# Loads and stores one a slot, four units split twice, weight sums on VectorE instead of GpSimd

## What is computed

```python
mod = silu(c) @ w_ada + b_ada; shift, scale, gate = split(mod, 3)
h = rmsnorm(x, g_pre) * (1 + scale) + shift
p = h @ w_in                                  # 1024 x 8704, the bulk of the work
y_pool = pool_mixer(a_in) * silu(a_g)
y_hgrn = hgrn2_mixer(b_q, b_f, b_i) * silu(b_g)
y_conv = short_conv_mixer(c_x, c_b, c_c) * silu(c_g)
y_diff = diff_attention(d_q, d_k, d_v) * silu(d_g)
merged = sum(sigmoid(m_g[i]) * (y_i @ w_merge_i))
x = x + gate * rmsnorm(merged @ w_out, g_post)
```

## Time and profile before

| what | value |
|---|---|
| median of 3 runs | 2409.23 us (2408.41 to 2409.46) |
| time of the profiled execution | 2409.45 us |
| its span, first to last instruction | 2407.7 us |
| PE, PEld busy | 2245.6 us (93%), 1857.7 us (77%) |
| DVE, ACT, POOL busy | 1474.8, 1122.4, 847.1 us |
| DMA | 569.99 MB, mean 237 GB/s |

### The profile page before, as it was taken

One profiled execution on the slowest core, in us unless ns is written; L12 is line 12 of the kernel. 1 busy time (PEld: TensorE's weight loads), 2 busy tenths in 40 slices (PEclk: granted clock), 3 DMA queues, 4 the chain that ended last, 5 costly groups with the idle time before them and its releaser, 6 DMA issues. The chain is left out here.

```text
span 2407.7 us, 35100 instructions
## 1 busy us (share of the span) xinstructions
PE 2245.6 (93%) x11573; PEld 1857.7 (77%) x11573; DVE 1474.8 (61%) x2645; ACT 1122.4 (47%) x2388; POOL 847.1 (35%) x739
## 2 busy tenths in 40 slices
PE   3798999998999999898999999999999978899998
PEld 3586788887777778786888888878888856787886
DVE  7766777748888795314776666445555435375571
ACT  5543566635454444323656665433434334344351
POOL 1223333326565563101222223133424306363453
PEclk7898999999999999999999999999999989999999
DMA  7899888678877778988565665587877775465561
GB/s 266 297 355 354 285 252 263 233 252 300 271 247 264 253 246 275 345 254 265 160 189 171 171 179 159 169 277 234 248 238 251 219 259 225 146 231 194 186 227 61
DMA packets 340780, 569.99 MB, mean 237 GB/s; under 512 B 27360, under 2 KB 213120, under 8 KB 335744
## 3 DMA queue, kind: packets, MB, share of 16 engines
q1 hardware_dynamic: 306336, 443.04, 54.7%
q10 hardware_dynamic: 34272, 124.80, 16.6%
HBM read 336.53 MB, written 236.45 MB: 238 GB/s over the span
## 5 line engine op out<-in xcount | busy, mean ns | idle before, releaser
L1772 PE MATMUL gb<-h_hi,w_both 128*128 128x512 f32 x1904 | 784.5, 412 | 71.4 <-DVE o L1308 34.1
L1774 PE MATMUL gb<-h_hi,w_both 128*128 128x512 f32 x1904 | 753.8, 396 | 0.0
L1773 PE MATMUL gb<-h_lo,w_both 128*128 128x512 f32 x1904 | 751.6, 395 | 0.0
L1772 PEld LDWEIGHTS gb<-h_hi,w_both 128*128 128x128 f32 x1904 | 363.8, 191 | 155.8 <-issue 79.8
L1774 PEld LDWEIGHTS gb<-h_hi,w_both 128*128 128x128 f32 x1904 | 362.7, 191 | 80.4
L1773 PEld LDWEIGHTS gb<-h_lo,w_both 128*128 128x128 f32 x1904 | 364.9, 192 | 66.2
L999 ACT ACTIVATE o<-gb 128x512 f32<-128x512 f32 x272 | 161.7, 594 | 381.8 <-PE gb L1774 324.8
L863 POOL TENSOR_TENSOR C_prob<-C_prob,C_cf 128x512 f32<-128x512 f32 (+3 forms) x160 | 159.6, 1022 | 464.3 <-DVE C_cf L1416 460.0
L1064 ACT ACTIVATE C_prob<-C_sc,C_negm 128x512 f32<-128x512 f32 (+3 forms) x320 | 198.4, 622 | 223.0 <-DVE C_negm L1394 215.3
L1308 DVE TENSOR_TENSOR o<-gb,o 128x512 f32<-128x512 f32 x204 | 140.2, 688 | 225.8 <-PE gb L1774 205.2
L1298 DVE TENSOR_TENSOR w_both<-w,w_both 128x512 fp32r<-128x512 f32 x170 | 153.3, 902 | 109.8 <-ACT w_both L976 109.6
(11 more groups left out here) (239 smaller groups left out, 3745.0 us busy)
## 6 DMA issues: line engine op xcount, KB each, us to landing
wS_scratch<-w_both SPq DMA_DIRECT2D x238, 512.0 KB, 3.9
w_both<-wS_scratch ACTq DMA_DIRECT2D x238, 512.0 KB, 4.4
w<-in_w_in_dram SPq DMA_DIRECT2D x68, 512.0 KB, 5.4
gT_scratch<-o SPq DMA_DIRECT2D x128, 256.0 KB, 4.6
D_gate<-gT_scratch SPq DMA_DIRECT2D x32, 1024.0 KB, 5.2
pT_scratch<-o SPq DMA_DIRECT2D x80, 256.0 KB, 4.4
D_wm_stage<-wm_scratch SPq DMA_DIRECT2D x32, 640.0 KB, 6.1
C_qt<-qB_scratch SPq DMA_DIRECT2D x128, 128.0 KB, 3.6
```

Of the source, the lines that this page charges most:

```text
L1772: mm(to, hi[:, k, :], h_hi[j][:, k, :], start=(fresh and k == 0), stop=False, skip_group_check=True)
L1773: mm(to, hi[:, k, :], h_lo[j][:, k, :], start=False, stop=False, skip_group_check=True)
L1774: last = mm(to, lo[:, k, :], h_hi[j][:, k, :], start=False, stop=(k == KH - 1), skip_group_check=True)
```

## The change

The sums of weight blocks go from POOL's loop to DVE's, at the same slots (j = 4, 5, 6 of the unit before), behind `low`. Unit 0's sums stay with POOL, ahead of the loop. POOL's t3 and low parts of the second half also go to DVE, so that DVE makes all of them. The units 2 to 5 are no longer stored: in the second half of the tokens (slots 252 to 279) their weights are loaded from w_in again, summed and split again. Loads and stores that were issued together are spread: x tiles over slots 5 to 12, operands' stores one a slot, the first loads of an attention one a slot from 40 and from 270 on, four stage loads two and two. DVE's preparation of an attention goes to slots 45 and 275. In the second half's mixers the rounds are made two at a time, at offsets 0 and 4, and picked at 1, 2, 5, 6. The core of the diff:

```diff
+REMADE = range(2, 6)
-LOW_BY_VECTOR, LOW_BY_POOL = (0, 2, 3, 6), (1, 4, 5)
-BEGIN = ((39, 2), (279, 1))
+BEGIN = (40, 270)
+def made(n):
+    return n < KEPT or n // PER - NU in REMADE
+def stored(n):
+    return n < KEPT and n // PER not in REMADE
+def in_order(u):
+    return u if u < NU else u - REMADE[0]
+def made_before(n):
+    return n if n < KEPT else KEPT + sum(map(made, range(KEPT, n)))
+def ring_uses(n):
+    return sum(stored(m) or not made(m) for m in range(n % RING, n, RING))
...
+        def step_in(half, slot, offset):
+            i = mix_step(slot, offset)
+            return i if i is not None and i // MIX_HALF == half else None
+        def score_step(n, r):
+            i = step_in(0, n, 2 * r)
+            return step_in(1, n, (0, 0, 4, 4)[r]) if i is None else i
+        def pick_step(n, r):
+            i = step_in(0, n, 2 * r + 1)
+            return step_in(1, n, (1, 2, 5, 6)[r]) if i is None else i
...
             def begin_attention(half, part):
-                    for g in reversed(range(ng // 2, ng)):
-                        load_k(half, 0, g)
-                elif part == 1:
...
+                elif part <= ng:
+                    load_k(half, 0, ng - part)
+                elif part <= 2 * ng:
+                    load_v(half, 0, 2 * ng - part)
+                elif part < 2 * ng + QT:
+                    load_q(i + part - 2 * ng)
+                elif part < 2 * ng + QT + 2:
+                    load_silu(i + part - 2 * ng - QT)
...
@@ SP's loop
-                if n + LEAD - 1 < KEPT:
+                if stored(n + LEAD - 1):
                     store_weights(n + LEAD - 1)
-                if j == 1 and u + 1 < NU:
+                if j == 1 and made(PER * (u + 1)):
                     load_w1(u + 1)
-                if j == 4 and u + 2 < NU:
+                if j == 4 and made(PER * (u + 2)):
                     load_w2(u + 2)
...
-                    for t in range(8):
-                        load_x(1, t)
-                if n == PREP + 14:
-                    sp.wait_ge(*evicted(1, 3))
-                    store_operand(0, 0)
-                    store_operand(0, 1)
...
+                if PREP <= n < PREP + 8:
+                    load_x(1, n - PREP)
+                for kk in range(2):
+                    if n == PREP + 14 + kk:
+                        sp.wait_ge(*evicted(1, 2 * kk + 1))
+                        store_operand(0, kk)
...
+                    if n == PREP + 31 + kk:
+                        sp.wait_ge(t4_made, 3 + kk)
+                        store_operand(6, kk)
-                if n == PREP + 32:
+                if n == PREP + 34:
                     sp.wait_ge(post_ready, 2)
                     sp.dma_start(post_d, row).then_inc(post_stored, 16)
-                    part, odd = divmod(n - BEGIN[half][0], BEGIN[half][1])
-                    if not odd and 0 <= part < 5:
-                        begin_attention(half, part)
+                    if n >= BEGIN[half]:
+                        begin_attention(half, n - BEGIN[half])
...
-                    for m in range(STAGES):
+                    for m in range(2):
+                        load_stage(m)
+                if n == CHANGE[0] - 1:
+                    for m in range(2, STAGES):
                         load_stage(m)
...
@@ POOL's loop
-                u, j = divmod(n, PER)
-                if u + 1 < NU:
-                    if j == 4:
-                        sum_s3_s1(u + 1)
-                    if j == 5:
-                        sum_s2(u + 1)
-                    if j == 6:
-                        sum_s4(u + 1)
-                if n in (PREP + 26, PREP + 27):
-                    t3(n - PREP - 26)
-                for jj, slot in enumerate(CHANGE):
-                    if n == slot and jj in LOW_BY_POOL:
-                        for kk in range(2):
-                            low(jj, kk, stage[(2 * jj + kk) % STAGES])
...
@@ ACT's loop
-                if n + LEAD < KEPT:
-                    high(n + LEAD)
-                elif n + LEAD < PRODUCTS:
-                    load_weights(n + LEAD)
+                if n + LEAD < PRODUCTS:
+                    if made(n + LEAD):
+                        high(n + LEAD)
+                    else:
+                        load_weights(n + LEAD)
...
@@ DVE's loop
-                if n + LEAD < KEPT:
+                if n + LEAD < PRODUCTS and made(n + LEAD):
                     low(n + LEAD)
+                u, j = divmod(n, PER)
+                if made(PER * (u + 1)):
+                    if j == 4:
+                        sum_s3_s1(in_order(u + 1))
+                    if j == 5:
+                        sum_s2(in_order(u + 1))
+                    if j == 6:
+                        sum_s4(in_order(u + 1))
...
-                    t4(1, n - PREP - 28)
+                    t3(1, n - PREP - 28)
+                if n in (PREP + 30, PREP + 31):
+                    t4(1, n - PREP - 30)
-                if n == PREP + 30:
+                if n == PREP + 32:
                     finish_row()
                 for jj, slot in enumerate(CHANGE):
-                    if n == slot and jj in LOW_BY_VECTOR:
+                    if n == slot:
...
-                    if n == ATTENTION[half][0]:
+                    if n == BEGIN[half] + 5:
                         begin_attention(half)
...
-                    i = mix_step(n, 2 * r + 1)
+                    i = pick_step(n, r)
@@ PE's loop
-                    i = mix_step(n, 2 * r)
+                    i = score_step(n, r)
                     if i is not None:
                         rounds(i, r)
```

More of the change, by code:

```diff
@@ L346, in lo_count @@
         def lo_count(half, j, kk):
[L347 to L351, removed]
+            return h_lo_ready, hi_count(half, j, kk)
         packed = x_in[0]
@@ L966, in high @@
                 u, j = divmod(n, PER)
+                u = in_order(u)
                 if n >= RING:
                     act.wait_ge(product_done, n - RING + 1)
-                    act.wait_ge(w_kept[n % RING], 16 * (n // RING))
+                    if ring_uses(n):
+                        act.wait_ge(w_kept[n % RING], 16 * ring_uses(n))
                 if j == 0:
@@ L1296, in low, with sum_s3_s1, sum_s2, sum_s4 @@
             def low(n):
-                dve.wait_ge(whi, n + 1)
+                dve.wait_ge(whi, made_before(n) + 1)
                 tt(w_lo[n % RING][:, :, :], source(n), w_hi[n % RING][:, :, :].bitcast(F32), ALU.subtract).then_inc(wlo, 1)
+            def sum_s3_s1(u):
+                if u:
+                    dve.wait_ge(wlo, PER * (u - 1) + 5)
+                dve.wait_ge(w1_loaded, 16 * (u + 1))
+                tt(s3[:, :, :], w1[:, :, 0:P], w1[:, :, P:2 * P], ALU.subtract).then_inc(s_made, 1)
+                dve.wait_ge(w2_loaded[u % 2], 16 * (u // 2 + 1))
+                dve.wait_ge(s_made, 4 * u + 1)
+                tt(w1[:, :, P:2 * P], w1[:, :, P:2 * P], w2[u % 2][:, :, P:2 * P], ALU.add).then_inc(s_made, 1)
+            def sum_s2(u):
+                dve.wait_ge(s_made, 4 * u + 2)
+                tt(s2[:, :, :], w1[:, :, P:2 * P], w1[:, :, 0:P], ALU.subtract).then_inc(s_made, 1)
+            def sum_s4(u):
+                dve.wait_ge(s_made, 4 * u + 3)
+                dve.wait_ge(wlo, PER * u + 2)
+                tt(w2[u % 2][:, :, 0:P], w2[u % 2][:, :, 0:P], s2[:, :, :], ALU.subtract).then_inc(s_made, 1)
             def add_out(n):
@@ L1351, in t2_, with t3 @@
                 tt(parts(t2, kk), parts(h22, kk), parts(h11, kk), ALU.subtract).then_inc(t2_made, 1)
-            def t3_first(kk):
-                dve.wait_ge(t1_made, 2)
+            def t3(half, kk):
+                if half:
+                    dve.wait_ge(*evicted(1, 15))
+                dve.wait_ge(t1_made, 2 * half + 2)
                 tt(parts(h12, kk), parts(h22, kk), parts(h12, kk), ALU.subtract).then_inc(t3_made, 1)
@@ L1366, in low_h @@
                 dve.wait_ge(h_hi_ready, hi_count(half, j, kk))
-                tt(parts(h_lo[j], kk), src, parts(h_hi[j], kk).bitcast(F32), ALU.subtract).then_inc(h_lo_v, 1)
+                tt(parts(h_lo[j], kk), src, parts(h_hi[j], kk).bitcast(F32), ALU.subtract).then_inc(h_lo_ready, 1)
             def add_row(k):
@@ L1761, in product @@
                 if part == 0:
-                    if n < KEPT:
-                        pe.wait_ge(wlo, n + 1)
+                    if made(n):
+                        pe.wait_ge(wlo, made_before(n) + 1)
                     else:
-                        pe.wait_ge(w_kept[n % RING], 16 * (KEEPS[n % RING] + (n - KEPT) // RING + 1))
+                        pe.wait_ge(w_kept[n % RING], 16 * (ring_uses(n) + 1))
                     if u % NU == 0:
```

86 lines of the change are left out of this document (30 added, 56 removed).

## The result

The changed kernel takes **2386.07 us** (median of 4 runs, 2381.21 to 2387.18) against 2409.35 for the kernel before on the same chip: 23 us less, ratio 0.990 with the interval 0.988 to 0.991. The forecast was 2356. The sign was right and the time lies inside the range, but of the 53.5 us forecast 23 came. Of the rivals B ("mixers keep their stall", 2378) came nearest.

A forecast was written before the change was run, and what follows sets the result against it. PE, busy 93% of the 2407.7 us span, was taken as the bound, with stalls from full DMA and DVE-POOL interference. Terms -18, -14, -2, -2, -10, -2, -5.5 sum to -53.5, giving 2355.7 us, range 2330 to 2388.

The forecast's parts named there:

- Rival B: First mixers: DVE as full as before, its late work still holds PE, attention costs 4 us; 2378 us, chance 0.14.
- part 1: Weight sums moved from POOL to DVE: -18 of 30.8 us in the first mixers, 0 in first attention and startup.
- the sign that would prove it wrong: Among the signs listed as wrong: ACT's splits waiting for DVE's sums.
- The first attention: Slots 50 to 117: sums on DVE cost 0 (bounds -3, +8), covered by DVE's 79 us of slack.
- Parts 2 and 3: Slots 13 to 50: t3 and lows to DVE, four units split twice relieving DMA; together -14 us (bounds -8, -19).
- Part 4: Loads one a slot: -2 us in slots 5 to 13, -2 in the change of operands, -10 at second attention's begin.
- Parts 5 and 6: Begin of first mixers loses POOL's interference, -2 us; second mixers' rounds two by two save idle weight loading, -5.5 us.
- The rule on the shared pair: Lock on the DVE and GpSimd pair for whole instructions: return to DVE nearer 70 us; forecast kept about half, 33.
- Rival D: First mixers and attention: DVE becomes the bound, nothing returns for the added sums; +23 us, 2433 us, chance 0.06.

The follow-up runs named there:

- changed, second trace: The changed kernel run again unaltered, beside other runs on one chip: median 2384.3 us.
- experiment 11: Changed kernel with sums one slot early on DVE, but on GpSimd for the first attention's units and units 26, 27, 30, 31, 32: 2373.1 us.
- Experiments 1 and 10: Changed kernel with all sums back on GpSimd: 2378.5 us; with sums on GpSimd in the first attention only, elsewhere on DVE one slot early: 2371.7 us.
- experiment 6: Changed kernel with no unit split twice, so 28 more stores and 28 more loads of split blocks: 2399.5 us.
- experiment 9: Changed kernel with sums back on GpSimd, loads and stores in bursts and rounds two slots apart again: 2406.1 us.
- experiment 7: Changed kernel with the spreading undone, loads and stores in bursts and DVE's attention preparation back in slots 50 and 284: 2402.9 us.

## Why the prediction was wrong in size

**The step that failed is part 1, in its second half.** Its first half held: "DVE stays at 262 us" came out at 263.6. Both sides of that balance were sized low, the sums by 41.6 against 33 (priced at 0.69 us from an undisturbed row, while GpSimd's mixer work goes on beside them at 823 to 920 ns) and the return by 39.5 against 33, and they cancelled. What failed is the next inference, that with the same load "the bursts in which DVE falls a slot behind" vanish, 18 of 30.8 us. Between kernels the first mixers follow DVE's load:

| kernel | DVE busy | stretch |
|---|---|---|
| before | 261.5 | 318.5 |
| changed | 263.6 | 314.9 |
| sums on GpSimd | 262.4 | 315.8 |
| sums cut | 235.1 | 299.8 |
| GpSimd cut | 223.1 | 294.2 |
| changed, second trace | 265.4 | 317.6 |
| sums a slot earlier | 264.9 | 312.7 |
| experiment 11 | 260.4 | 319.4 |

15.0 us for 28.5 of DVE, 20.7 for 40.5: half a microsecond for each, down towards PE's floor of 288. Where the load is about equal the time scatters by 7 us, from 312.7 to 319.4, and not by load; none comes near the 300 forecast. ACT's wait for GpSimd (10.7 us) went as foreseen, and a wait for DVE's sum (20.9) took its place, which the prediction had named as the sign that would prove it wrong. I had checked that s2 is made a slot ahead of ACT's need by the program's order, not where DVE's queue would be by then. So the wait was called hidden without a look at the queue. Rival B had the mechanism, at a chance of 0.14: DVE as full as before, its late state update and late outputs holding PE as before, part 1 giving nothing, the attention costing 4 us.

**The first attention** was given as 0, bounds -3 and +8, with the slack of 79 us as cover. It cost 7.0. The slack is an average; the maxima of the scores come in a chain from PE to DVE to ACT, and a sum in DVE's queue delays that chain. PE's wait for ACT's C_prob rose from 1.4 us to 7.4, before and after:

```profile
PE C_sc L1841 <- ACT C_prob L1064: 1.4, 3, 1.0
PE C_sc L1878 <- ACT C_prob L1070: 7.4, 6, 2.4
```

Experiments 1 and 10 gave the 7 us back by the sums alone.

**Together** these two are 14.4 + 7 = 21 of the 25 us by which the first trace missed its sum of -53.5.

**Parts 2 and 3** (-14): -10.4 to slot 50. The mechanism is shown (DMA from 1.00 to 0.78 in slots 13 to 40, PE without a wait), and by experiment 6 it is part 3's. What remains is 120.5 - 111.8 = 8.7 us where I had left 5, and 6.9 of it lies in slots 40 to 50, where the stores are back and ACT waits 8.8 us for one of o. The same begin costs more further on: slots 40 to 58 give 2.4 us back with the loads spread and 6.6 in experiment 9.

**Part 4**: second attention -9.6 for -10, with the mechanism shown. For slots 5 to 13, "not one byte leaves it" was wrong as a reason though the table's -1.5 looks right: experiment 7 puts 5.2 us on the spreading there, and 1.7 MB leave the stretch for the next. That -1.5 came near -2 is luck. The gain of slots 5 to 13 was partly hidden because the stretch ahead of it shifted too: with the sums on GpSimd slots 0 to 5 take 35.2 and 5 to 13 take 27.1, 62.3 in all against 60.8. Slots 0 to 5 take 28.8 to 30.9 us in every trace with the sums on DVE and 33.0 to 35.2 in those with them on GpSimd, so the startup's gain came with part 1. DVE's preparation in slot 45, which the forecast gave no term, was worth some of the attention's begin: PE's wait for it is 1.4 us before and none after.

**Parts 5 and 6**: -1.9 for -2 and -5.2 for -5.5. The change of operands rose by 1.5 us (slots 226 to 237, 32.5 us; 31.0 with the sums on GpSimd), so part 1 cost there too.

**The rule on the shared pair** (the Trainium skill, SBUF — State Buffer, section SBUF: two separate sides), read as the whole length of each sum, would have returned nearer 70 us; 39.5 came back, between the row's half and that whole. Rival D's page (the Trainium skill, Perfetto Trace Analysis, section Optimizing Scalar/DVE Operations) says that moving work off a saturated DVE, even to GpSimd, may make sense, and that between those two it might not help. In the mixers, where DVE is fullest, it was a draw; in the attention, where DVE is not full on average, having the sums on GpSimd was worth 7 us.

## What to carry to other kernels

Moving work from GpSimd to VectorE trades a cost that VectorE pays in longer instructions for one that it pays in more of them: work out both, the moved instruction at the duration it has beside GpSimd's *remaining* work, and if the load comes out equal expect the time to be equal, whatever waits disappear. A wait on a busy engine's queue does not go away because its releaser moved to another busy queue. An engine with slack on average can still stand in a short chain, so put the moved work where no such chain runs: here on GpSimd in the attention and one slot early on VectorE elsewhere, 13 to 14 us better than the change as made.

## What was not expected of the hardware

- With DMA full in both, slots 5 to 13 took 37.2 us with eight loads issued together (0.98, 353 GB/s) and 32.0 one a slot (1.00, 357 GB/s): the spread loads carried 1.7 MB on into slots that had room.
- A two-input VectorE instruction of 128x1 took 153 to 160 ns (median over the run) and 266 to 287 on the mean in the first mixers, where some met GpSimd's work; one of 128x512 took 684. Cut to one column the sums still cost a third of their 41.6 us.
- Cutting GpSimd's work beside VectorE in the first mixers from 125.0 us to 35.7 shortened VectorE's by 40.5 us; taking the sums away, 69.1 us of GpSimd by their four lines before, had shortened it by 39.5.
- A VectorE state update of 128x128 took 0.35 us alone and up to 2.3 us beside a 128x896 instruction of GpSimd: at 655.27 us two of them take 3.90 us, until 659.17, and GpSimd's two 128x896 instructions run from 654.23 to 659.03.
